# From the router to the first expert turns of a hybrid decoder layer on one core: transposes, last norm, row picks and piece loads in another order

## What is computed

```python
x = x + memory_cross_attention(rms_norm(x, ...), ...)          # ends with the projection by xattn_wo
ht = rms_norm(x, ffn_norm_g)
p_coarse = softmax(ht @ w_coarse + b_coarse); grp = argmax(p_coarse)          # 4 groups
fine = (ht @ w_fine + b_fine) of that group; top_p, top_i = top_k(softmax(fine), 2)   # 2 of 4 experts
for e in range(16):                                            # combine is 0 for experts not chosen
    y = y + combine[:, e] * ((silu(ht @ w_gate[e]) * (ht @ w_up[e])) @ w_down[e])
out = rms_norm(x + y, final_norm_g)
```

## Time and profile before

| | before |
|---|---|
| median of 3 runs | 787.72 us (787.14 to 789.12) |
| the profiled execution | 787.38 us |
| its span, first to last instruction | 785.5 us |
| mean granted TensorE clock | 0.988 |
| PE, DVE, ACT, POOL busy | 96%, 68%, 58%, 23% |
| the chain that ended last | PE 93%, DVE 3% |

### The profile page before, as it was taken

How to read it: one execution, slowest core, us unless ns; L and a number is a source line. 1 busy time by engine, 2 the same in 40 slices (tenths; PEclk the granted TensorE clock), 3 DMA queues, 4 the chain that set the end, 5 groups by cost and what they waited for, 6 DMA issues and landing times.

```text
span 785.5 us, 11565 instructions
## 1 busy us (share of the span) xinstructions
PE 751.7 (96%) x4124; PEld 582.1 (74%) x4124; DVE 537.3 (68%) x711; ACT 456.9 (58%) x665; POOL 179.9 (23%) x185
## 2 busy tenths in 40 slices
PE   4999999999999999999999969999999999999994
PEld 3978789777788889888788844677777777777763
DVE  5445378598782455622555488599989889899986
ACT  4455662487883236433443242587887887787862
POOL 3800023000001011000000100135555444555312
PEclk9999999999999999999999989999999999999997
DMA  9934521000405435542104768999999999999942
GB/s 297 233 94 141 155 83 59 1 2 2 161 3 188 134 108 177 172 151 66 53 1 143 310 236 321 398 380 381 383 370 373 382 372 375 380 384 384 385 154 107
DMA packets 61902, 166.88 MB, mean 212 GB/s; under 512 B 8224, under 2 KB 36192, under 8 KB 49576
## 3 DMA queue, kind: packets, MB, share of 16 engines
q1 hardware_dynamic: 56376, 150.69, 51.8%
q0 software_dynamic: 4480, 12.48, 6.8%
q10 hardware_dynamic: 1008, 3.21, 1.2%
HBM read 153.44 MB, written 12.85 MB: 212 GB/s over the span
## 4 chain that ended last, share of the span: by engine, by line
PE 93%; DVE 3%; DMA 1%; ACT 1%; issue 1%; POOL 0%; SPq 0%; POOLq 0%; ACTq 0%; DVEq 0%
PE ps L1976 24%; PE ps L1978 23%; PE ps L1977 23%; PE ps L2249 3%; PE ps L2197 3%; PE ps L2175 2%; PE ps L2444 2%; PE ps L2287 2%; PE ps L2178 1%; PE ps L2108 1%; PE ps L2424 1%; PE ps L2366 1%; DMA raw<-in_w_in 1%; PE ps L2179 1%; PE ps L2430 1%
## 5 line engine op out<-in xcount | busy, mean ns | idle before, releaser
L1356 DVE TENSOR_TENSOR wlo<-raw,whi 128x2048 fp32r<-128x2048 f32 x29 | 66.5, 2292 | 78.5 <-ACT whi L878 78.4
L1976 PE MATMUL ps<-whi,mhi 128*96 128x512 f32 (+1 forms) x276 | 110.1, 399 | 2.0 <-DVE mlo L1909 1.2
L1978 PE MATMUL ps<-whi,mlo 128*96 128x512 f32 (+1 forms) x276 | 109.3, 396 | 0.0
L1977 PE MATMUL ps<-wlo,mhi 128*96 128x512 f32 (+1 forms) x276 | 108.8, 394 | 0.0
L1371 DVE TENSOR_TENSOR wlo<-arena,whi 128x2048 fp32r<-128x2048 f32 x39 | 89.4, 2291 | 20.4 <-ACT whi L897 20.4
L741 POOL TENSOR_SCALAR stat<-stat 128x1 f32<-128x1 f32 x18 | 11.3, 630 | 355.9 <-ACT tok L903 209.4
L897 ACT ACTIVATE whi<-arena 128x2048 fp32r<-128x2048 f32 x39 | 74.7, 1915 | 26.4 <-PE ps L1978 26.4
L878 ACT ACTIVATE whi<-raw 128x2048 fp32r<-128x2048 f32 x29 | 55.4, 1910 | 48.5 <-PE ps L1978 48.4
L1976 PE MATMUL ps<-ahi,whi 128*128 128x512 f32 x192 | 75.6, 394 | 0.0
L1978 PE MATMUL ps<-ahi,wlo 128*128 128x512 f32 x192 | 74.8, 390 | 0.0
L1977 PE MATMUL ps<-alo,whi 128*128 128x512 f32 x192 | 74.8, 390 | 0.0
(11 more groups left out here) (396 smaller groups left out, 1692.4 us busy)
## 6 DMA issues: line engine op xcount, KB each, us to landing
arena<-in_exp_w_gate SPq DMA_DIRECT2D x30, 1024.0 KB, 14.4
arena<-in_exp_w_up SPq DMA_DIRECT2D x17, 1024.0 KB, 14.2
raw_a<-in_exp_w_down SPq DMA_DIRECT2D x16, 1024.0 KB, 15.2
raw<-in_exp_w_up SPq DMA_DIRECT2D x15, 1024.0 KB, 13.3
arena<-in_exp_w_down SPq DMA_DIRECT2D x9, 1024.0 KB, 18.6
raw<-in_exp_w_down SPq DMA_DIRECT2D x7, 1024.0 KB, 15.1
raw<-in_w_in SPq DMA_DIRECT2D x5, 1024.0 KB, 7.3
raw<-in_w_in SPq DMA_DIRECT2D x10, 512.0 KB, 5.6
```

The costliest lines, as they stand in the source:

```text
L1356: v.tensor_tensor(wlo[:, n % SPLIT, :], raw[:, n % RAW, :], whi[:, n % SPLIT, :].bitcast(F32), ALU.subtract).then_inc(lo_done, 1)
L1976: mm(out_, ahi_, bhi_, start=first, stop=False)
L1977: mm(out_, ahi_, blo_, start=False, stop=False)
L1978: return mm(out_, alo_, bhi_, start=False, stop=last)
```

## The change

- **PE:** tile 0 is transposed after group 1 of xo3, tile 1 after group 2, tile 2 in the middle of group 3, tile 3 in the middle of the router matmuls of tiles 0 and 1. Those of tiles 2 and 3 run in two halves of the contraction, each after its half of `norm_lo`.
- **The last norm tile:** ACT scales X of tile 3 into tok, and POOL multiplies it by the gain into H3; DVE's `norm_last(3)` is gone.
- **Picks:** for tiles 0 and 1, ACT makes a rounded copy mhi of H3 and POOL the rest mlo; the pick is then two fp32r matmuls (first_hot of these tiles is fp32r too) in place of one float32 matmul. Tiles 2 and 3 stay as they were. The first half takes the tiles in the order 0, 2, 1, 3.
- **First turn:** chunk 1's rows are transposed ahead of piece 3, and he of chunk 0 after the first two gate pieces of turn 1. That turn is written out; the loop begins at turn 2.
- **Splits:** the split of piece 7 (and the one that answers to it in later turns) moves from the head of a turn to the end of the turn before, ahead of the branch.
- **Loads:** pieces 12 to 17 are issued ahead of the wait for route_done, with fixed expert numbers (chunks 1 to 3 are always of experts 1 to 3); the loop's two halves change places.

```diff
@@ first_hot
-        first_hot = work[:, 2096:2096 + NT * CHUNK].rearrange("p (t s) -> p t s", t=NT)
+        hot_r = wrt2[:, :, :].rearrange("p k n -> p (k n)")[:, 0:2 * CHUNK].rearrange("p (t s) -> p t s", t=2)
+        hot_f = work[:, 2096:2096 + NT * CHUNK].rearrange("p (t s) -> p t s", t=NT)
+        first_hot = [hot_r[:, t, :] if t < 2 else hot_f[:, t, :] for t in range(NT)]
@@ SP
+            for i, (w, e) in enumerate(((wu, 2), (wu, 2), (wd, 1), (wd, 1), (wg, 3), (wg, 3))):
+                sp.wait_ge(lo_done, ND + i + 1)
+                if i < 4:
+                    sp.wait_ge(used, i + 1)
+                load_expert(w, e, i % 2, RING + i)
             sp.wait_ge(route_done, 1)
...
-                load_middle(2 * h, RING)
                 load_middle(2 * h + 1, MRAW)
-            load_middle(2 * pairs, RING)
+                load_middle(2 * h + 2, RING)
@@ POOL, after rms of the last tile
+            pool.wait_ge(gain_full, 64)
+            pool.wait_ge(h_done, N4 - 1)
+            pool.wait_ge(pick_act, 1)
+            lanes = "t (q k) -> t q k"
+            pool.tensor_tensor(H3[:, NT - 1, :].rearrange("t (k q) -> t q k", k=KD), tok[:, 2, :].rearrange(lanes, k=KD),
+                               gbc[:, :].rearrange(lanes, k=KD), ALU.mult).then_inc(h_done, 1)
+
+            for t in range(2):
+                pool.wait_ge(pick_act, t + 2)
+                pool.tensor_tensor(mlo[:, D * t:D * (t + 1)], H3[:, t, :], mhi[:, D * t:D * (t + 1)].bitcast(F32), ALU.subtract)\
+                    .then_inc(pick_lo, 1)
@@ ACT
             router_out(0)
             square_last(3)
             router_out(1)
+            act.wait_ge(rms_done, N4)
+            a.activation(tok[:, 2, :], X[:, NT - 1, :], ACT.Copy, scale=stat[:, 2, N4 - 1:N4]).then_inc(pick_act, 1)
+            for t in range(2):
+                act.wait_ge(h_done, N3 + t + 1)
+                a.activation(mhi[:, D * t:D * (t + 1)], H3[:, t, :], ACT.Copy).then_inc(pick_act, 1)
             split_expert(4)
             split_expert(5)
@@ DVE
             evacuate(ND - 1, (0, 1))
             norm_last(0)
+            norm_lo(N3, alo, ahi, 0)
             evacuate(ND - 1, (2,))
+            norm_lo(N3 + 1, alo, ahi, 1)
             norm_last(1)
-            norm_lo(N3, alo, ahi, 0)
             evacuate(ND - 1, (3,))
-            for t in range(1, NT):
-                norm_lo(N3 + t, alo, ahi, t)
+            norm_lo(N3 + 2, alo, ahi, 2)
+            norm_lo(N3 + 3, alo, ahi, 3)
             norm_last(2)
...
-            norm_last(3)
             dve.wait_ge(r_exp, 2)
@@ PE, pick
-                return mm(ps[4 + b][0:CHUNK, :], first_hot[:, t, :], H3[:, t, 512 * b:512 * b + 512],
-                          start=(t == 0), stop=(t == NT - 1))
+                out_, c = ps[4 + b][0:CHUNK, :], slice(D * t + 512 * b, D * t + 512 * b + 512)
+                if t < 2:
+                    mm(out_, first_hot[t], mhi[:, c], start=(t == 0), stop=False)
+                    pe.wait_ge(pick_lo, t + 1)
+                    return mm(out_, first_hot[t], mlo[:, c], start=False, stop=False)
+                return mm(out_, first_hot[t], H3[:, t, 512 * b:512 * b + 512], start=False, stop=(t == NT - 1))
```

More of the change, by code:

```diff
@@ L489, in build @@
         h_done = sem("h_done")
+        pick_act = sem("pick_act")
+        pick_lo = sem("pick_lo")
         ntp_done = sem("ntp_done")
@@ L700, in load_turn @@
                     sp.wait_ge(lo_done, 6 * (j - 2) + (ND + i + 1))
-                    if i < 4 and m0 == RING:
-                        sp.wait_ge(used, i + 1)
                     load_expert(w, e, i % 2, m0 + i)
@@ L1224, in _ @@
             act.wait_ge(PX.pv_done, PX.njobs)
-            for t in range(3):
-                square_last(t)
-            for t in range(NT):
-                norm_hi(N3 + t, ahi, t)
+            square_last(0)
+            square_last(1)
+            norm_hi(N3, ahi, 0)
+            norm_hi(N3 + 1, ahi, 1)
+            square_last(2)
+            norm_hi(N3 + 2, ahi, 2)
+            norm_hi(N3 + 3, ahi, 3)
             router_out(0)
@@ L1281, in _ @@
             xg_hi_out(2)
+            split_expert(7, 0)
             he_hi_out(1)
@@ L1289, in turn @@
                 base = RING * h + (at + 4)
-                split_expert(at + 7, h)
                 split_expert(at + 8, h)
@@ L1313, in turn @@
                     he_hi_out(j + 1)
+                    split_expert(at + 13, h)
             with act.Fori(0, pairs) as h:
@@ L1802, in _ @@
             for t in range(NT):
-                v.tensor_scalar(first_hot[:, t, :], siota, rank[:, t, 0:1], R[:, 636 + t:637 + t],
+                v.tensor_scalar(first_hot[t], siota, rank[:, t, 0:1], R[:, 636 + t:637 + t],
                                 ALU.is_equal, ALU.mult).then_inc(first_done, 1)
             v.tensor_copy(cnt, ps[2][:, 0:NEXP]).then_inc(first_done, 1)
-            norm_last(3)
             dve.wait_ge(r_exp, 2)
@@ L1913, in _ @@
             split_expert(6)
+            xg_lo_out(2)
             gated(1, 4)
-            xg_lo_out(2)
+            split_expert(7, 0)
             he_lo_out(1)
@@ L1921, in turn @@
                 at, j = MRAW * r, 2 * h + (1 + r)
-                for m in (7, 8, 9, 10):
+                for m in (8, 9, 10):
                     split_expert(at + m, h)
@@ L2031, in dense @@
                             kk = KF * c0 + k
+                            if (ORDER[n], idx, k) == ("xo3", NT - 1, KF // 2):
+                                norm_transposes(N3 + 2, X[:, 2, :])
                             ins = three(bank[:, :], xh[:, kk, tc], xl[:, kk, tc], h4[:, k, :], l4[:, k, :],
@@ L2034, in dense @@
                         ins.then_inc(grp_done, 1)
-                        if (ORDER[n], idx) == ("xo3", 2):
-                            norm_transposes(N3, X[:, 0, :])
+                        if ORDER[n] == "xo3" and 0 < idx < NT - 1:
+                            norm_transposes(N3 + idx - 1, X[:, idx - 1, :])
                         continue
@@ L2115, in _, with narrow @@
             dense(1)
-            def narrow(bank, w2, n, t0, w):
-                for k in range(KD):
+            def narrow(bank, w2, n, t0, w, ks=range(KD)):
+                for k in ks:
                     x_hi, x_lo = ahi[:, k, t0:t0 + w], alo[:, k, t0:t0 + w]
@@ L2338, in _ @@
                 dense(n)
-            for t in range(1, NT):
-                norm_transposes(N3 + t, X[:, t, :])
             pe.wait_ge(sm_lo, 2)
-            pe.wait_ge(evac["dve"], evacs(len(groups) - 1, "dve"))
+            pe.wait_ge(evac["dve"], evacs(of_piece[ND - 1][1], "dve"))
+            pe.wait_ge(ntp_lo, 2 * (N3 + 2))
+            narrow(ps[0], wrt2, ROUT_W, 0, 2 * P, range(KF))
+            norm_transposes(N3 + 3, X[:, 3, :])
+            narrow(ps[0], wrt2, ROUT_W, 0, 2 * P, range(KF, KD)).then_inc(route_mm, 1)
             for b in range(2):
-                pe.wait_ge(ntp_lo, 2 * (N3 + 2 * b + 2))
-                narrow(ps[b], wrt2, ROUT_W, 2 * P * b, 2 * P).then_inc(route_mm, 1)
+                pe.wait_ge(ntp_lo, 2 * (N3 + NT) + b - 1)
+                ins = narrow(ps[1], wrt2, ROUT_W, 2 * P, 2 * P, range(KF * b, KF * b + KF))
+            ins.then_inc(route_mm, 1)
             for b in range(2):
@@ L2375, in picked_transposes @@
                 ins.then_inc(xg_tp, 1)
-            for t in range(NT):
+            pe.wait_ge(pick_act, 3)
+            for t in (0, 2, 1, 3):
                 pe.wait_ge(first_done, t + 1)
@@ L2435, in _ @@
                 pe.wait_ge(first_in, min(m, 1) + 1)
+                if m == 3:
+                    pe.wait_ge(xg_in, 16)
+                    xg_transposes()
                 full, need = moe_full(m)
@@ L2447, in _ @@
                     lists()
-            pe.wait_ge(xg_in, 16)
-            xg_transposes()
-            pe.wait_ge(he_done, 2)
-            he_transposes()
             pe.wait_ge(route_done, 1)
@@ L2454, in _, with turn @@
             turns = 2 * pairs
-            def turn(j, last):
+            def turn(j, last, first=False):
                 n0 = 6 * (j - 1) + (NMP + 1)
@@ L2462, in turn @@
                 pe.wait_ge(he_done, j + 1)
+                if first:
+                    he_transposes()
                 for m in range(2):
@@ L2475, in turn @@
                 he_transposes()
-            with pe.Fori(1, turns + 1) as j:
+            turn(1, False, True)
+            with pe.Fori(2, turns + 1) as j:
                 turn(j, False)
```

## The result

| | before | after |
|---|---|---|
| median | 787.58 us (10 runs, 785.28 to 789.12) | 790.96 us (10 runs, 789.53 to 793.43) |
| the profiled execution, its span | 787.38, 785.5 us | 790.27, 788.4 us |
| mean granted TensorE clock | 0.988 | 0.986 |
| PE, DVE, ACT, POOL busy | 96%, 68%, 58%, 23% | 95%, 69%, 58%, 24% |

After over before is 1.0045, with a 95% interval of 1.0032 to 1.0059: **slower by 0.45%, some 3.4 us**, where 785.2 was forecast, in a range from 781.6 to 787.6. Turn 1 starts 4.36 us later than before (498.58 against 494.22) and gives 1.45 of that back; the rest reaches the end. The turns run as before: PE is busy for all of 500 to 600 at full clock (100.00, as in the earlier trace rows).

The account below looks back on a forecast made before the run. It took PE, busy 96%, as the bound, with savings only in PE work, idle time and half-clock stretches. Turn 1's 0.5 plus the clock's 1.7 made 2.2 off 787.38: 785.2 us, range 781.6 to 787.6.

Parts of the forecast that it names:

- Last norm off DVE: norm_last(3), 1.97 us, leaves DVE, so the tables for lists end near 476.3; ACT's extra copies cost nothing.
- Picks: Tiles 0 and 1 as fp32r pairs: 1.6 us less at full clock; low clock again to about 470.4; POOL operations 2.2 each.
- Rows of chunk 1: Transposes ahead of piece 3: PE arrives at 486.0, gather takes 8.7 us and lands at 489.3, PE waits 3.3.
- a gain of about 4 us that nobody asks for: Early loads: pieces go out earlier, gaining the loads about 4 us, though the 9 in hand already suffice.
- Transposes: Two sets moved between projection groups: the DVE chain starts at 459.65 against 460.39, 0.7 us gained, bounds 0 and 1.7.
- Turn 1: Starts at 493.4 instead of 494.22, net 0.5 us; following piece 3 without a gap avoids the low clock, 1.7 more.
- the other moves: Splits ahead of the branch, turn written out, loop's halves: same instructions in the same places of a turn, nothing gained.
- Rival A: The gather lands in time: with 6 us the wait is 0.6 and the gain 2.7 greater, 782.5; chance 0.35.
- Rival B: The clock falls in the wait for rows, so piece 3 and turn 1 pay 1.7 again: 786.9; chance 0.22.
- Rival C: Slower by POOL: operations of 4.4 us each make PE's picks wait for the rests: 790.8; chance 0.07.
- Rival D: Weights bound the turns, so an earlier start is given back before the end: 787.4; chance 0.03.
- The clock's gain of 1.7: With no gap between piece 3 and turn 1, the second stretch of low clock goes: 1.7 us.

Follow-up runs that it names:

- e4: Kernel before, plus nine POOL memsets of 896 columns beside the routing chain, which read nothing: 787.28 us, ratio 1.0002.
- e6: Changed kernel with the DVE chain's second operands and the masks' compare numbers in PSUM, pieces 12 to 17 loaded behind route_done: 785.76 us, ratio 0.9982.
- e9: e6 with piece 11 also issued behind the first gather: 784.15 us, ratio 0.9960.
- e10: e6 with pieces 10 and 11 both issued behind the first gather: 783.54 us (6 runs), ratio 0.9950.
- e1: Changed kernel without POOL's three operations and ACT's three copies: last norm on DVE, eight float32 picks, early loads kept: 788.43 us, ratio 1.0016.
- e11: e1 with pieces 12 to 17 loaded behind route_done and the gathered rows' transposes behind piece 3 again: 785.46 us, ratio 0.9976.
- e2: Changed kernel, POOL's and ACT's work kept, with the DVE chain's logits, masked scores and candidates in PSUM: 790.13 us, ratio 1.0041.
- e3: Kernel before, plus four POOL subtractions of 768 columns beside the routing chain, result unused: 791.80 us (4 runs), ratio 1.0069.
- e8: e1 with pieces 12 and on issued only once POOL has issued the first gather: 784.37 us, ratio 0.9960.
- e7: Changed kernel with only the loads of pieces 12 to 17 put back behind route_done: 787.99 us, ratio 1.0012.

## Why the prediction was wrong

The forecast lay 5.8 us below the median. Step by step:

- *Last norm off DVE*, "Price nothing": **the step that failed.** It costed POOL's work by its own length and DVE's relief, and left out the DVE operations that run beside it. The same holds for the two rests of *Picks*, which were weighed only by when POOL would be done with them. The length was nearly right: 2.37 and 2 x 2.34 against 2.2. What the three cost is 5.98 us of DVE's chain, one stalled operation for each (2.1 beside the multiply, 3.9 beside the rests), and those operations are on the path: PE waits 11.0 us for the one-hots (5.0 before). The Trainium skill has the rule, in SBUF — State Buffer, "Who interferes with whom": DVE with two SBUF inputs contends with a GpSimd instruction that reads SBUF, not with one that only writes it, and the later one is blocked to the end; `tensor_reduce` never contends. The runs agree for the chain's operations in each point: 2.27 against 0.17 us, e4's memsets, the reduce of 0.22. It spoke against this change, and the prediction did not weigh it.
- *Picks*, "1.6 less" at full clock, low clock to 470.4: the low clock moved with the idle time, to about 476.3 (a clock of 0.87 over 475 to 480 is 1.3 us at half speed). The picks' part is in b: 1.17 less. With no stall and the split picks kept (e6, e9, e10), b is 14.3 to 14.8 against 15.6 to 16.6 in the runs with float32 picks. That fits 1.6; the low clock's share in b differs from run to run, so it is not measured by itself.
- *Rows of chunk 1*, 8.7 and a wait of 3.3: the change itself gave 7.7 and 2.5, and e1, where nothing else was in the way, 8.55 and 3.3. The mechanism was right, and the size within 1 us. What the sum made of it was not: "a gain of about 4 us that nobody asks for" is the loads' side, and the price of 3.0 to 4.2 us for them was in the sum only as the difference between two ways the change could go, not as a part that could be left out.
- *Transposes*, 0.7: from the set of transposes that follows group 2 to the first DVE operation it is 10.53 now (448.93 to 459.46) and was 12.09 (448.30 to 460.39), with one set of 0.87 done earlier now: 12.09 - 10.53 - 0.87 = 0.69. Right.
- *Turn 1*: piece 3 runs into turn 1 without a gap, and no low clock follows; d is 1.45 less, about the 1.7 less 0.33 for he's transposes that was forecast. Right for this profile. The sum gives nothing for "the other moves"; the order of DVE's rests and `gated` was not among its terms. It is worth some 0.5 where the rows come behind piece 3 (e11) and is hidden under piece 3 in the change.
- Rival A (0.35) did not come: the gather was not in time. Rival B came not in the profiled execution but in e1 and e2. Rival C gave 790.8, near the 790.96 measured, by a mechanism that was not there: POOL's operations took 2.3, not 4.4, and PE never waited for a rest. Rival D did not come: the shift of 2.9 us at turn 1's transposes of rows (510.04 against 507.13) reached the end (spans 2.9 apart), as forecast of the turns. With b and c the forecast's path was nearly met (14.4 and 14.3 by its times, 14.55 and 13.63 measured); a was taken as unchanged, and its 5.98 us are more than the whole miss of 5.1 against the profiled execution.

The clock's gain of 1.7 was also counted whole, from one profiled execution. In e3 and e4, which leave that place as it was, piece 3 is followed by the same idle time, and no low clock came behind it: c is 13.15 in both, d 11.34 and 11.35, where before had 12.91. Before's runs spread over 785.0 to 789.1. Of the 94 that were run beside the experiments, 15 have a mean clock of 0.991 instead of 0.987 to 0.989 and take 785.0 to 785.7, as e4's profiled execution does (0.991, 786.02). So most runs of before may well pay the 1.7, but no profile shows in how many.

A gather with piece 12 ahead of it is late by its packets, as the DMA view of e1 shows (14 of 112 by 487, 4 us after its issue, and six still behind 489). The Trainium skill, DMA: Bandwidth & Descriptors, "Queues, rings and completion order", says that an engine goes round its queues packet by packet. That agrees with the 106 packets that started before piece 12 had landed; it did not save the gather from 8.55 us, as rival A had it.

What stays open is why the first packets start later with piece 12 ahead, and why the last ones straggle. Why the clock falls in some idle stretches of 2.5 to 3.3 us and not in others was not tried either.

## What to carry to other kernels

Before an operation is moved to POOL, list what DVE does at that time: an operation there with two SBUF inputs may stand still until POOL's is done, and if DVE is on the path, the move costs up to the full length of the POOL operation instead of nothing. If the work has to be on POOL, one operand of each such DVE operation in PSUM takes the collision away (5.05 against 10.94 us here); the masks, with one SBUF input, needed theirs in PSUM too. And a load issued early is not free for a short transfer that is issued behind it and waited for: issue the short one first (4.1 us here, e8 against e1). And look at each part of a change alone, since two losses in a row partly hide each other.

## What the hardware showed beyond expectation

- A DVE operation of 0.17 us took 2.27 beside a POOL operation that reads SBUF, and 0.17 beside POOL memsets; the masks (tensor_scalar, SBUF to SBUF, 96 columns) were held up by both: the first two took 2.65 instead of 0.57 in e2, all four 1.62 instead of 1.05 in e4, and 1.23 with no hold-up when they read from PSUM in e6 beside the same POOL work.
- A POOL tensor_tensor of 128x1024 takes 2.34 to 2.37 us, one of 768 columns 1.83, a memset of 128x896 0.85.
- The gather of 96 rows took 4.3 and 4.5 us with almost no other packets beside it (e3, e7), 4.9 to 6.7 with piece 10 or 10 and 11 issued 3.7 to 6.2 us ahead, 5.7 with these two 1.3 us behind it (e10), and 7.7 to 10.1 with piece 12 issued 1.4 to 2.3 us ahead of it.
